# A 48-row contraction for the broadcast matmuls, and matmuls in place of transposes that spread a column, in a three-layer transformer kernel

## The reference, cut to what matters

```python
# layer 1: the logits get the cumulated forget gates, one row per head
logits = einsum('bhqd,bhkd->bhqk', qb, k) * scale
logits = logits + cb[..., :, None] - c[..., None, :]
...
# every norm needs mean and 1/deviation of each token, spread over all features
y = (xf - mu) * lax.rsqrt(var + LN_EPS)
...
# layer 2: each head's output is divided by its own root mean square
o = o * lax.rsqrt(jnp.mean(jnp.square(o), axis=-1, keepdims=True) + RMS_EPS)
...
# layer 3: the decay between positions l and s, for 16 heads and two directions
seg = a_cs[..., :, None] - a_cs[..., None, :]
decay_in = jnp.exp(jnp.where(tri, seg, -jnp.inf))
```

## Time and profile before

| | |
|---|---|
| median of 3 runs | 2283.9 us (2275.99 to 2285.17) |
| the profiled execution | 2275.99 us, span 2274.2 us |
| granted TensorE clock, mean | 0.969 of full speed |
| TensorE busy | 2149.9 us, 95% of the span |
| VectorE, ScalarE, GpSimd busy | 1160.6, 1005.7, 945.0 us |
| transposes that change | 80 (16 in `stat1`, 32 in `stat3`, 32 in `dno`) |
| matmuls whose contraction is cut | 48 (16 in `nb`, 32 in `sh`) |

### The profile page before, as it was taken

How to read it: one execution, slowest core, us unless ns; L and a number is a source line. 1 busy time by engine, 2 the same in 40 slices (tenths; PEclk the granted TensorE clock), 3 DMA queues, 4 the chain that set the end, 5 groups by cost and what they waited for, 6 DMA issues and landing times.

```text
span 2274.2 us, 27791 instructions
## 1 busy us (share of the span) xinstructions
PE 2149.9 (95%) x10632; PEld 1789.4 (79%) x10640; DVE 1160.6 (51%) x1852; ACT 1005.7 (44%) x2030; POOL 945.0 (42%) x714
## 2 busy tenths in 40 slices
PE   7999899999998898899999999889999999999997
PEld 6888778888877777778888878778678887888886
DVE  3545565554343668465554354666854326444322
ACT  5666444443224566244443245656543234332222
POOL 3655563343446665453433343222413344222233
PEclk9999999999998989899999998999999999999998
DMA  4111122322222221122222211101012231222221
GB/s 162 56 56 56 56 93 96 108 93 104 87 87 79 83 76 61 52 79 93 93 99 98 102 63 68 44 32 56 19 66 88 89 111 63 104 94 106 90 102 53
DMA packets 29843, 183.04 MB, mean 80 GB/s; under 512 B 3984, under 2 KB 4112, under 8 KB 11920
## 3 DMA queue, kind: packets, MB, share of 16 engines
q1 hardware_dynamic: 29712, 181.27, 23.2%
HBM read 174.97 MB, written 2.10 MB: 78 GB/s over the span
## 4 chain that ended last, share of the span: by engine, by line
PE 83%; DVE 7%; ACT 4%; issue 4%; POOL 3%; DMA 0%; SPq 0%; POOLq 0%; DVEq 0%; ACTq 0%
PE PS L1486 80%; POOL LO L2779 1%; PE PS L1611 1%; DVE bQS L2228 1%; PE PS L1724 0%; POOL bTQ L2837 0%; POOL bROT L2832 0%; DVE aQS L2228 0%; DVE T_f L2300 0%; DVE YH L2330 0%; DVE bP L2532 0%; PE PS L1659 0%; ACT HI L1810 0%; ACT bP L2028 0%; DVE XL L2305 0%
## 5 line engine op out<-in xcount | busy, mean ns | idle before, releaser
L2779 POOL TENSOR_TENSOR LO<-RAW,HI 128x512 fp32r<-128x512 f32 (+2 forms) x382 | 542.7, 1437 | 609.4 <-ACT HI L1810 609.4
L1486 PE MATMUL PS<-XH,HI 128*128 128x512 f32 (+1 forms) x1584 | 638.4, 403 | 25.8 <-DVE XL L2228 7.1
L1486 PE MATMUL PS<-XH,LO 128*128 128x512 f32 (+1 forms) x1584 | 626.3, 395 | 0.0
L1486 PE MATMUL PS<-XL,HI 128*128 128x512 f32 (+1 forms) x1584 | 618.9, 395 | 0.0
L1810 ACT ACTIVATE HI<-RAW 128x512 fp32r<-128x512 f32 (+3 forms) x668 | 366.0, 607 | 171.4 <-PE PS L1486 168.1
L2228 DVE TENSOR_TENSOR LO<-RAW,HI 128x512 fp32r<-128x512 f32 (+2 forms) x286 | 304.1, 1068 | 246.0 <-ACT HI L1810 245.6
L1486 PEld LDWEIGHTS PS<-XH,HI 128*128 128x128 f32 (+1 forms) x1584 | 302.5, 191 | 89.7 <-issue 21.7
L1486 PEld LDWEIGHTS PS<-XH,LO 128*128 128x128 f32 (+1 forms) x1584 | 302.0, 191 | 65.8 <-issue 1.3
L1486 PEld LDWEIGHTS PS<-XL,HI 128*128 128x128 f32 (+1 forms) x1584 | 301.2, 191 | 61.4 <-DVE XL L2305 1.4
L1486 PE MATMUL PS<-HL,HI 128*128 128x512 f32 x528 | 205.7, 390 | 0.0
L1486 PE MATMUL PS<-HH,HI 128*128 128x512 f32 x528 | 205.7, 390 | 0.0
(11 more groups left out here) (409 smaller groups left out, 3289.0 us busy)
## 6 DMA issues: line engine op xcount, KB each, us to landing
RAW<-wall SPq DMA_DIRECT2D x138, 1024.0 KB, 4.8
RAW<-wall SPq DMA_DIRECT2D x24, 896.0 KB, 4.5
bROT<-bTQ SPq DMA_DIRECT2D x64, 64.0 KB, 2.0
RAW<-wall SPq DMA_DIRECT2D x5, 512.0 KB, 3.3
XF<-xT SPq DMA_DIRECT2D x4, 512.0 KB, 5.7
outT<-XR SPq DMA_DIRECT2D x8, 256.0 KB, 2.0
FP<-cfp SPq DMA_DIRECT2D x1, 1024.0 KB, 7.1
MKF<-cmask SPq DMA_DIRECT2D x1, 704.0 KB, 11.2
```

The lines of the kernel that those rows point to most:

```text
L1486: return e.matmul(out, a, b, start=start, stop=stop)
L2779: return e.tensor_tensor(out, x, h.bitcast(F32), ALU.subtract)
```

## The change

The stationary and moving operands of the 48 broadcast matmuls shrink from 128 to 48 partitions; `aNC` and `RF` are made 48 partitions high; zeros are written to 32 of their partitions instead of 128, from a zero column of the identity, so that `fz4` no longer waits for the constants; one of the three copies that fill `SEL` goes. The 80 transposes of repeated columns become plain float32 matmuls with the same two operands.

```diff
-    aNB, aNC = sb("aNB", 1024, F32, 4608), sb("aNC", 512, F32R, 4608 + 4 * K)
+    aNB, aNC = sb("aNB", 1024, F32, 4608), sb("aNC", 512, F32R, 4608 + 4 * K, 48)
...
-    RF = sb("cRF", 1024, F32R, R0 + 117 * K)
+    RF = sb("cRF", 1024, F32R, R0 + 117 * K, 48)
...
# stat1, and in the same way stat3 (RSD into PS[6]) and dno (bMS into its bank)
-                    m = e.transpose(PS[5][:, 128 * c:128 * c + 128], MU[:, c:c + 1].to_broadcast([128, 128]), IDN)
+                    m = mm(PS[5][:, 128 * c:128 * c + 128], MU[:, c:c + 1].to_broadcast([128, 128]), IDN)
...
# nb
-                mm(PS[bank][:, :], SEL[:, h:h + 1].to_broadcast([128, 128]), aNC[:, :]).then_inc(SEM["nb"], 1)
+                mm(PS[bank][:, :], SEL[0:48, h:h + 1].to_broadcast([48, 128]), aNC[:, :]).then_inc(SEM["nb"], 1)
...
# sh
-                    mm(PS[b][:, :], SEL[:, h:h + 1].to_broadcast([128, 128]), RF[:, 512 * dr:512 * dr + 512], True, False)
+                    mm(PS[b][:, :], SEL[0:48, h:h + 1].to_broadcast([48, 128]), RF[:, 512 * dr:512 * dr + 512], True, False)
...
# cst
-                act(SEL[32:64, :], IDN[32:64, 32:48], ACT.Copy)
-                act(SEL[64:128, :], IDN[64:128, 0:16], ACT.Copy).then_inc(SEM["ca"], 1)
+                act(SEL[32:48, :], IDN[32:48, 32:48], ACT.Copy).then_inc(SEM["ca"], 1)
...
# fz4
-                e.wait_ge(*when("cd", "cst"))
-                act(aNC[:, :], NEGC[:, 8:9].to_broadcast([128, 512]), ACT.Copy).then_inc(s_av, 1)
+                act(aNC[0:32, :], IDN[0:32, 64:65].to_broadcast([32, 512]), ACT.Copy).then_inc(s_av, 1)
...
# rf
-                act(r, NEGC[:, 8:9].to_broadcast([128, 512]), ACT.Copy).then_inc(s_av, 1)
+                act(r[0:32, :], IDN[0:32, 64:65].to_broadcast([32, 512]), ACT.Copy).then_inc(s_av, 1)
```

More of the change, by code:

```diff
@@ L1581, in tensor @@
                 for c in range(4):
-                    m = e.transpose(PS[6][:, 128 * c:128 * c + 128], RSD[:, c:c + 1].to_broadcast([128, 128]), IDN)
+                    m = mm(PS[6][:, 128 * c:128 * c + 128], RSD[:, c:c + 1].to_broadcast([128, 128]), IDN)
                 m.then_inc(SEM["spr"], 1)
@@ L1683, in tensor @@
                 for c in range(4):
-                    m = e.transpose(PS[bank][:, 128 * c:128 * c + 128], bMS[:, 4 * h + c:4 * h + c + 1].to_broadcast([128, 128]), IDN)
+                    m = mm(PS[bank][:, 128 * c:128 * c + 128], bMS[:, 4 * h + c:4 * h + c + 1].to_broadcast([128, 128]), IDN)
                 m.then_inc(SEM["dbc"], 1)
```

## The result

The changed kernel is slower: 2297.95 us against 2283.15 us (medians of four runs each), 14.8 us more. The ratio on record is 1.0069, with a 95% interval from 1.0051 to 1.0087, so 11.6 to 19.9 us. The forecast was 2293 us, with 2280 to 2300 as its range; the time lies inside, but on the slower side, to which the prediction gave 0.31, and not in the middle case, to which it gave 0.63. The profiled execution after has a span of 2284.7 us, which is 10.5 us over the one before. It is shorter than every timed run of this kernel (fourteen are on record, the shortest with a span of 2292.2 us), and its mean granted clock is higher, 0.975 where theirs is 0.968 to 0.972. So the two traces serve to compare places with each other, and not to size the whole.

The account below looks back on a forecast made before the run. TensorE, busy for 95% of the span, was taken to bound the kernel; 3.1 + 5.7 + 0.9 = 9.7 us on the median of 2283.9 gave 2293.6, stated as 2293 us, range 2280 to 2300.

Parts of the forecast that it names:

- the middle case: Whole kernel: neither slower nor faster by the 0.5%, 11.4 us, that a measurement can tell from no change; chance 0.63.
- the rival by which all of it counts: Both broadcast stretches: nothing is covered by waits; 4.5 + 9.0 + 2.4 = 15.9 us, 2300 us; chance 0.15.
- Streaming at 48 rows: The 48 broadcast matmuls: fewer contraction rows bring no gain in streaming time, 0.
- The price of a switch: TensorE at each change to or from a 48-row block: 0.14 us lost, bounds 0 and 0.14.
- the rival without a hole: Broadcast matmuls: a 48-row block costs no switch, like `rf`'s narrow block; 2285 us; chance 0.27.
- Layer 1: Gate broadcasts (`nb`): two switches each, eleven of 16 uncovered by waits; 3.1 us, bounds 0 and 4.5.
- Layer 3: Decay broadcasts (`sh`): 9.0 us of switches put in, 2.6 to 9.0 left after waits; middle taken, 5.7 us.
- The sign that the prediction named: Profile of the changed kernel: the layer 1 and layer 3 broadcast stretches longer together by some 9 us.
- Float32 matmuls for transposes: `stat1`, `stat3` and `dno`: small extra mainly at the head of groups after idleness; 0.9 us, bounds 0.1 and 2.4.
- The clock rival: Norms and `dno`: plain matmuls keep the clock up where transposes do not; 2268 us, or 2277 with holes; chance 0.06.

Follow-up runs that it names:

- e3: Kernel before with 80 rows instead of 128 in the 48 broadcast matmuls, nothing else changed; ratio 1.0001 (0.9989 to 1.0013).
- e9: Kernel before with 48 rows only in the 16 gate broadcasts of layer 1; ratio 1.0011 (0.9997 to 1.0024), 2.5 us.
- e2: Kernel before with float32 matmuls in place of the 80 transposes, nothing else changed; ratio 1.0041 (1.0027 to 1.0055), 9.4 us.
- e5: Kernel before with each of the 80 transposes issued twice into the same place; ratio 1.0033 (1.0019 to 1.0047), 7.5 us.
- e1: Kernel before with 48 rows instead of 128 in the 48 broadcast matmuls, nothing else changed; ratio 1.0015 (1.0004 to 1.0027), 3.4 us.
- e10: Kernel before with 48 rows only in the 32 decay broadcasts of layer 3; ratio 0.9990 (0.9976 to 1.0004).
- e12: Kernel before with layer 3's broadcast and mask matmuls each cut into two of 256 columns, still 128 rows; ratio 0.9986 (0.9970 to 1.0003).

## Why the prediction was right, and where it was not

**The size of the whole** was forecast at 9.7 us and came out at 14.8 by the medians. One term was far too small and none too large by as much. That the time still lies in the range is in part luck: the range reached to 2300 for the sake of the rival by which all of it counts, and what made up the difference was something else, the second pass, which no rival had. A small slip is in the sum as well: the middle between 2.6 and 9.0 is 5.8, not 5.7.

**Streaming at 48 rows: right.** No gain; with 80 rows (e3) nothing changes that a run shows, and with 48 the stretches get longer, not shorter.

**The price of a switch: right.** 0.14 us from `cp2`, 0.145 measured in both stretches. The choice of `cp2` over `rf` was the one that mattered, and the rival without a hole is out. The Trainium skill's rule that changing the tiling mode drains TensorE ("TensorEngine Tiling (Array Packing)", Key Properties) fits 48 and 32 rows and the 64 columns of `cp2`, and the 80 rows, more than the 64 of that mode, which bring no hole. It does not fit the 16 columns of `rf`, which bring none either; there the measurement decides.

**Layer 1: right.** 3.1 us forecast. e9 gives 2.5. From the first gate broadcast to the last it is 192.4 us in the kernel before and 195.9 in the changed one, 3.5 more, with a granted clock of 0.99 in both; at a clock of 0.97 it is 195.4 without the holes (e3) and 198.5 with them (e9), 3.1 more.

**Layer 3: the cover was right, the clock was not foreseen.** The middle of 5.7 us stands beside 4.2 at equal clock over the runs and 4.1 in the traces. The sign that the prediction named, both stretches longer together by some 9 us, came out at 6.9 (3.5 in layer 1, and 139.4 to 142.8 in layer 3 of the changed kernel), where the clock in layer 3 was 0.99 before and 1.00 after. In plain time the part cost nothing that its run shows.

**Float32 matmuls for transposes: ten times too small.** The step that failed is the sentence "Float32 matmuls of the same shape: eight in 1.16". Those eight records are four matmuls, `cb`'s, for one of its two groups; the code has eight and the trace 16. I counted records, divided by them, and found a pace of 0.112 us, which is that of one pass; the second pass was put at nothing. The right price of one is 0.22 at full clock. The passes put in are 80 x 0.11 = 8.8 us at full clock and more at half; 9.4 were measured, where 0.9 stood in the sum with a bound of 2.4. The same slip is in the description ahead of the prediction: `cp2` has eight float32 matmuls, recorded as sixteen. It did no harm there, since the estimate of the hole rested on starts and eight recorded pairs.

**The rival that all of it counts** came nearest in time (2300 us) and is wrong as a mechanism. **The clock rival** is out: with plain matmuls in place of transposes (e2) the mean clock was 0.9683 against 0.9678. The passes were also twice as many there, but e5 has as many of them as transposes, and its mean clock was 0.9684 against 0.9672 beside it, so matmuls in place of transposes did not raise the clock. The Trainium skill's rule that transpose mode does not count as busy for the clock ("TensorE: Matmul & The Clock Gate", Part 4) would give the matmuls the higher clock; these runs show no such effect.

**The parts:** e1 and e2 are 3.4 + 9.4 = 12.8 us by their ratios (6.5 + 9.6 = 16.1 at equal clock), inside the 11.6 to 19.9 of the whole. Brought to equal clock in the same way, the whole is some 18.5 (fourteen runs, mean 2297.6 us at 0.9697, against the 87 runs of the kernel before, 2282.8 at 0.9673), though these stood on different chips. The fills, the dropped copy and the dropped wait were not run by themselves; they lie in what is left between the sum and the whole, which the intervals do not separate from nothing.

None of the runs is a version that is clearly faster than the kernel before; e10 and e12 have medians 3 and 5 us under it, with intervals that reach past 1.

## What to carry to other kernels

Before a duration is taken from a group of rows, compare the group's count with the count in the code: a record may be a pass and not an instruction of yours. Cutting a contraction from 128 rows to 48 or 32 bought no time here and cost a hole at each change of block size; if it must be, put the small blocks together. And where the busiest engine still waits for others, extra work on it is paid only in part at first (4 of 9.3 us) and in full with the second dose. The first even looked free, because the granted clock differed: so compare a stretch between the same two instructions, and at like clock, before calling a dose free.

## What the runs showed of the hardware that was not expected

- A plain float32 matmul of 128 by 128 is recorded as two matmuls 0.11 us apart at full clock (0.21 at half), a transpose of the same data as one. With 512 columns the two are 0.43 us apart (`cXW`,`cBT` at 1580.68 in the kernel before), where a float32r matmul steps by 0.23: nearly four times the price in all.
- Blocks of 32 and 48 rows bring a hole of 0.145 us at each change of size, and so do `cp2`'s blocks of 64 columns; blocks of 80 rows and of 16 columns do not. In the changed kernel, early in the span, the first full block behind the 16-column ones starts at the normal step of 0.23 us:

```profile
14.74 0.39 PE L1486 MATMUL PS<-XH,LO 128*16 128x512 f32 x1
14.97 0.39 PE L1486 MATMUL PS<-XH,HI 128*128 128x512 f32 x1
```

- Why 16 columns at the array's edge bring no hole and 64 do is open.
- The kernel's own spread, 2275 to 2292 us over 29 runs, goes with the mean granted clock, 1.6 us for each 0.001. Kernels with one and the same arithmetic differed in it by up to 0.004.
